# Gated linear attention with interleaved cross-attention: another order of the chains, and repeated gate-logit matmuls in the last two heads

## The reference, cut to what matters

```python
log_a = log_sigmoid(glr @ w_gate2 + b_gate) / 16        # glr: rank 16; this product is the gate logits
b = cumsum(log_a within a chunk of 64); b_ref = b[31]; b_last = b[63]
att = tril((q * exp(b - b_ref)) @ (k * exp(b_ref - b)).T)
o = att @ v + (q * exp(b)) @ state
state = exp(b_last) * state + (k * exp(b_last - b)).T @ v
tok = rms_norm(o) * silu(og)
p = softmax(xq @ k_mem.T / 8); xa = p @ v_mem            # cross-attention
x = x + concat(tok, xa) @ w_out
```

## Time and profile before

| what | value |
|---|---|
| median of 3 runs | 2727.84 us |
| lowest, highest run | 2727.36, 2731.31 us |
| the profiled execution | 2724.89 us, its span 2723.1 us |
| mean granted TensorE clock over the span | 0.977 of full speed |
| TensorE busy | 2603.9 us, 96% of the span |
| VectorE, ScalarE, GpSimd busy | 1317.6, 848.3, 200.5 us |

### The profile page before, as it was taken

The page is one execution under the profiler, slowest core; times in us unless marked ns, Lnnn a source line. Parts: engine busy times, 40 slices in busy tenths (PEclk is TensorE's granted clock), DMA queues, the critical chain, the costliest instruction groups (busy, mean ns, idle before and its releaser), DMA issues. The chain is left out here.

```text
span 2723.1 us, 33041 instructions
## 1 busy us (share of the span) xinstructions
PE 2603.9 (96%) x12444; PEld 2206.9 (81%) x12444; DVE 1317.6 (48%) x2290; ACT 848.3 (31%) x1774; POOL 200.5 (7%) x271
## 2 busy tenths in 40 slices
PE   7998888999999999998999999998899999999999
PEld 7996767878888888887888888787778888888887
DVE  4423453445444544446554562453645544454445
ACT  6434342332222222214425433324333222222221
POOL 1100131000000000001211021111000000000000
PEclk9999978999999999998999999998999999999999
DMA  4221201121111111112102001102421111111111
GB/s 145 87 70 28 87 15 39 39 87 50 51 47 46 51 50 46 46 39 101 47 17 74 32 32 50 59 17 80 154 71 55 47 54 54 46 52 49 46 39 62
DMA packets 165245, 153.88 MB, mean 57 GB/s; under 512 B 32856, under 2 KB 135496, under 8 KB 165128
## 3 DMA queue, kind: packets, MB, share of 16 engines
q1 hardware_dynamic: 160968, 152.31, 17.5%
q10 hardware_dynamic: 4160, 0.02, 0.1%
HBM read 134.69 MB, written 17.61 MB: 56 GB/s over the span
## 5 line engine op out<-in xcount | busy, mean ns | idle before, releaser
L356 PE MATMUL psum<-hT_hi,f_up_hi 128*128 128x512 f32 x1376 | 426.6, 389 | 3.9 <-PEq L562 3.9
L356 PE MATMUL psum<-hT_hi,f_up_lo 128*128 128x512 f32 x1376 | 426.3, 389 | 0.0
L356 PE MATMUL psum<-hT_lo,f_up_hi 128*128 128x512 f32 x1376 | 426.2, 389 | 0.0
L238 DVE TENSOR_TENSOR f_up_lo<-raw,f_up_hi 128x1024 fp32r<-128x1024 f32 x84 | 102.9, 1225 | 489.7 <-ACT f_up_hi L182 489.7
L356 PEld LDWEIGHTS psum<-hT_hi,f_up_hi 128*128 128x128 f32 x1376 | 258.1, 188 | 58.5 <-issue 5.1
L356 PEld LDWEIGHTS psum<-hT_hi,f_up_lo 128*128 128x128 f32 x1376 | 258.3, 188 | 53.7
L356 PEld LDWEIGHTS psum<-hT_lo,f_up_hi 128*128 128x128 f32 x1376 | 258.3, 188 | 53.5
L256 DVE TENSOR_TENSOR XY<-XY,psum 128x512 f32<-128x512 f32 x352 | 234.4, 684 | 113.9 <-PE psum L52 113.7
L182 ACT ACTIVATE f_up_hi<-raw 128x1024 fp32r<-128x1024 f32 x84 | 89.1, 1061 | 613.7 <-PE psum L356 589.0
L50 PE MATMUL psum<-w_hi,hT_hi 128*128 128x512 f32 (+1 forms) x640 | 249.7, 390 | 17.2 <-DVE w_lo L805 10.7
L50 PE MATMUL psum<-f_down_hi,f_act_hi 128*128 128x512 f32 x640 | 249.0, 389 | 0.0
(11 more groups left out here) (289 smaller groups left out, 4055.0 us busy)
## 6 DMA issues: line engine op xcount, KB each, us to landing
raw<-in_ffn_w_up_dram SPq DMA_DIRECT2D x88, 512.0 KB, 3.7
f_down_raw<-in_ffn_w_down_dram SPq DMA_DIRECT2D x22, 1024.0 KB, 4.9
w_raw<-in_b_w_in_dram SPq DMA_DIRECT2D x18, 1024.0 KB, 5.4
w_raw<-in_a_w_in_dram SPq DMA_DIRECT2D x8, 768.0 KB, 5.7
group_out<-stage SPq DMA_DIRECT2D x24, 256.0 KB, 2.1
o_outs<-group_out SPq DMA_DIRECT2D x24, 256.0 KB, 3.7
XY<-in_x_dram SPq DMA_DIRECT2D x8, 512.0 KB, 10.3
w_raw<-in_xa_w_kv_dram SPq DMA_DIRECT2D x8, 512.0 KB, 3.6
```

The costliest lines, as they stand in the source:

```text
L238: nc.vector.tensor_tensor(up_lo[n_slot][:, :, :], up_raw[n_slot], up_hi[n_slot][:, :, :].bitcast(F32), ALU.subtract).then_inc(up_split, 1)
L356: mm = nc.tensor.matmul(psum[:, 2 * j + half, :], w[j][:, d, :], h[:, d, half * HALF:(half + 1) * HALF], start=first, stop=final)
```

## The change

- `CrossUnits`: the output products of a unit go to a bank of the ring in place of bank 3, and each unit (not each two) has its reciprocal and its division. The transposes are in bank 3. The buffers of the probabilities lie in `cross_room`, a piece of SBUF that was the split weights' second buffer, with one still in V.
- `project`: all parts from 2 on use one pair of weight buffers and banks 0 and 1 (before: two pairs, and banks 0, 1 or 2, 3). A part starts after ACT has copied the one before (before: the one two before).
- ACT: `gate` is cut in `gate_in` and `gate_out`, with the copies of the token products between them; a head's odd part is copied and split later, and in head h the cross-attention's exponentials of stage "att" stand behind the copies of the key rows.
- DVE: `cross_pair` and the cross-attention steps of "att" stand ahead of the next head's `sums_of`; `states` and the steps of "state" stand ahead of `product(h + 1, 0)`; the third product stands behind `outputs`.
- TensorE: 4 slices (before 3) of an even part are projected ahead of the gate; the steps of "state" stand ahead of the odd part; cross steps are dealt out 3, 2, 3, 3, 2, 3, 3.
- `fill(n)`: n matmuls of head 0's gate weights with the rank rows into bank 2, which nobody reads: 2, 2, 3 and 3 at four places of head 2 and of head 3, 20 in all.

```diff
-    def pe(self, pe, s):
+    def pe(self, pe, s, ring_wait):
...
-            if i == 0 and t >= 1:
-                pe.wait_ge(self.out_done, t)
+            ring_wait(u)
...
-        CROSS = {(1, "out"): range(0, 3), (2, "att"): range(3, 6), (2, "state"): range(6, 9), (2, "out"): range(9, 12),
-                 (3, "att"): range(12, 14), (3, "state"): range(14, 16), (3, "out"): range(16, CrossUnits.STEPS)}
+        CROSS = {(1, "out"): range(0, 3), (2, "att"): range(3, 5), (2, "state"): range(5, 8), (2, "out"): range(8, 11),
+                 (3, "att"): range(11, 13), (3, "state"): range(13, 16), (3, "out"): range(16, CrossUnits.STEPS)}
...
         @block.vector
...
             product(0, 0)
             product(0, 3)
-            low(3)
             product(0, 1)
             product(0, 2)
             for h in range(GLA_HEADS):
                 more = h + 1 < GLA_HEADS
-                if more:
-                    sums_of(h + 1)
+                fresh = h + 1 < LAST
                 cross_pair(h)
                 cross_steps(cross.dve, dve, h, "att")
                 if more:
+                    sums_of(h + 1)
+                if fresh:
+                    low(2 * h + 3)
+                states(h)
+                cross_steps(cross.dve, dve, h, "state")
+                if more:
                     product(h + 1, 0)
-                states(h)
                 if h + 2 < LAST:
                     low(2 * h + 4)
                 if more:
                     product(h + 1, 1)
-                    product(h + 1, 2)
-                if h + 2 < LAST:
-                    low(2 * h + 5)
-                cross_steps(cross.dve, dve, h, "state")
                 outputs(h)
                 if more:
+                    product(h + 1, 2)
                     product(h + 1, 3)
...
          @block.tensor
...
             def project(s, ds=range(DC)):
-                h, part = divmod(s, 2)
+                w_hi, w_lo = (x[1 if s == 1 else 0] for x in (first_parts.hi, first_parts.lo))
                 if s >= 2:
                     pe.wait_ge(w_split, s - 1)
-                    pe.wait_ge(copied, s - 1)
+                    pe.wait_ge(copied, 1 if s == 2 else s)
...
+            def fill(n):
+
+                for i in range(n):
+                    nc.tensor.matmul(psum[0:DK, 2, :], gate2[:, 0:DK], rank[:, i % 2 * HALF:(i % 2 + 1) * HALF], start=True, stop=True)
+
-            EARLY = 3
+            EARLY = 4
...
             for h in range(GLA_HEADS):
                 if h + 1 < GLA_HEADS:
                     gate(h + 1)
+                if h + 2 > LAST:
+                    fill(2)
                 token_products(h)
                 if h + 1 < LAST:
                     project(2 * h + 2, range(EARLY, DC))
-                cross_steps(cross.pe, pe, h, "att")
+                cross_at(h, "att")
+                if h + 2 > LAST:
+                    fill(2)
                 state_changes(h)
+                cross_at(h, "state")
+                if h + 2 > LAST:
+                    fill(3)
                 if h + 1 < LAST:
                     project(2 * h + 3)
-                cross_steps(cross.pe, pe, h, "state")
                 outputs(h)
...
+                cross_at(h, "out")
                 if h + 2 < LAST:
                     project(2 * h + 4, range(EARLY))
-                cross_steps(cross.pe, pe, h, "out")
+                if h + 2 > LAST:
+                    fill(3)
```

More of the change, by code:

```diff
@@ L1359, in dve @@
         if 0 <= u < self.PAIRS:
+            two = slice(2 * u, 2 * u + 2)
             dve.wait_ge(self.turned, u + 1)
@@ L1478, in source, with enter, enter_cross, part_bank @@
             return (last_rows if h == LAST else qk_rows)[i][0:DK, :, :]
-        first_of, z_of = [], [0]
+        def enter(kind, who, n, h):
+            entry_of[h, kind] = len(ring)
+            ring.extend([(kind, who, h)] * n)
+        def enter_cross(h, stage):
+            for s in CROSS.get((h, stage), ()):
+                u = s - CrossUnits.O_LAG
+                if 0 <= u < CrossUnits.PAIRS:
+                    cross_of[u] = len(ring)
+                    ring.append(("xa", "xa", u))
+        enter("z", "act", 2, 0)
         for h in range(GLA_HEADS):
             if h + 1 < GLA_HEADS:
[L1483 to L1486, removed]
+                enter("z", "act", 2, h + 1)
+            enter("att", "act", 2, h)
+            enter("cross", "dve", 1, h)
+            enter_cross(h, "att")
+            enter("keys", "act", 2, h)
+            enter("delta", "state", 4, h)
+            enter_cross(h, "state")
+            enter("out", "dve", 4, h)
+            enter_cross(h, "out")
+        z_of = [entry_of[h, "z"] for h in range(GLA_HEADS)]
         def freed(i):
-            kind, who = ring[i]
+            kind, who, h = ring[i]
+            if kind == "xa":
+                return cross.out_done, h + 1
             if kind == "delta":
-                h = max(h for h in range(GLA_HEADS) if first_of[h] <= i)
-                return state_ready, (PAIRS - 1) * h + min(2 * (i - first_of[h] - 5) + 2, PAIRS - 1)
-            return (by_act if who == "act" else by_dve), sum(w == who for _, w in ring[:i + 1])
+                return state_ready, (PAIRS - 1) * h + min(2 * (i - entry_of[h, "delta"]) + 2, PAIRS - 1)
+            return (by_act if who == "act" else by_dve), sum(w == who for _, w, _ in ring[:i + 1])
         def bank(i):
             return psum[:, 4 + i % 4, :]
+        def part_bank(s, half):
+            return psum[:, (2 if s == 1 else 0) + half, :]
+        def at(h, kind, i=0):
+            return entry_of[h, kind] + i
         def mixes_before(i):
-            return sum(kind != "z" for kind, _ in ring[:i])
+            return sum(kind not in ("z", "xa") for kind, _, _ in ring[:i])
         block = ctx.enter_context(nc.Block())
@@ L1564, in high @@
             def high(s):
-                h, part = divmod(s, 2)
                 act.wait_ge(w_loaded, 32 * (s - 1))
-                act.wait_ge(projected, s - 1)
-                nc.scalar.activation(parts_hi[part], w_raw, ACT.Copy).then_inc(w_high, 1)
+                act.wait_ge(projected, 1 if s == 2 else s)
+                nc.scalar.activation(first_parts.hi[0], w_raw, ACT.Copy).then_inc(w_high, 1)
             def copy(h, i):
+                first = 2 if h == 0 and i == 1 else 0
                 act.wait_ge(projected, 2 * h + i + 1)
@@ L1626, in _ @@
                     factor(h + 1, 1)
-                    if fresh:
-                        copy(h + 1, 0)
-                if h:
-                    act.wait_ge(squared, PAIRS * h)
-                for i in range(2):
-                    act.wait_ge(mixed, mixes_before(f + 3 + i) + 1)
-                    nc.scalar.activation(k_rows[:, 4 * i:4 * i + 4, :], bank(f + 3 + i)[:, 0:4 * DK].rearrange("p (c k) -> p c k", k=DK),
-                                         ACT.Copy).then_inc(by_act, 1)
+                cross_steps(cross.act, act, h, "state")
+                if more:
+                    factor(h + 1, 2)
+                if fresh:
+                    copy(h + 1, 1)
                 if h + 2 < LAST:
                     high(2 * h + 4)
-                if more:
-                    factor(h + 1, 2)
-                    if fresh:
-                        copy(h + 1, 1)
-                if h + 2 < LAST:
-                    high(2 * h + 5)
-                cross_steps(cross.act, act, h, "state")
                 if h:
```

156 lines of the change are left out of this document (78 added, 78 removed).

## The result

The changed kernel takes **2752.8 us** (median of 4 runs, 2748.9 to 2757.8), the one before 2727.6 (2727.3 to 2731.3) beside it: a ratio of 1.009, 95% interval 1.0077 to 1.0102. It is **25.2 us slower**. The forecast had the sign right but said 10.8, and its range ended at 2744. The profiled execution took 2748.9 us, with a span of 2747.1 against 2723.1.

What follows compares the result with a forecast made beforehand. TensorE, busy nearly all through, was taken to bound the kernel. Heads 0 and 1 gave -5.0 us, the rest -4.8 + 17.2 + 0.7 + 2.7 = +15.8, together +10.8: 2737 us, range 2723 to 2744.

Steps and rivals of the forecast that it cites:

- I take it that the stretches cost what they cost before: Stretches at 1.2 GHz come to as much as before, so 5.5 us possibly gained in heads 2 and 3 is left out.
- warm: Rival: fills count as work and raise the clock in heads 2 and 3; -1.3 to -5.7 us, middle -3.5; chance 0.20.
- The fills' own length: Fills in heads 2 and 3, 0.9 us each at 2.4 GHz, covering no wait: +17.2, and +2.7 for the last three.
- The third product ... up to 1.22 us ... +0.7: Heads 2 and 3: product moved behind `outputs` lengthens the chain the wait of 5.99 hangs on; 0 to 1.22, middle +0.7.
- Heads 0 and 1: Terms up to the start of step 2 sum to -5.0 us (before at 337.96); new waits of 2.9 and twice 1.9.
- -4.7: Heads 0 and 1: clock falls at 257.4 and 308.6 cost 6.4 us and go; 1.7 us given back for new waits.
- if step 2 isn't about 5 us early: Test at the start of step 2: unless about 5 us early, at 333, the whole forecast falls.
- The product ahead of step 2: A product of 1.22 us moves behind `outputs`, into the chain that the wait of 4.98 hangs on: +1.2 us.
- Heads 2 and 3, waits: Waits of 3.60 and 2.04 shorten, the latter to one like 0.81; 1.91 left for the sums: -4.8 us.
- The buffer rival: Rival: one pair of weight buffers makes TensorE wait at parts 3 and 5; +15 us; chance 0.08.
- They fill: Rival: fills stand in waits missed in the reading and cost nothing at fifteen places; -8 us; chance 0.09.
- The next phase's transposes: Sign of being right: the phase after the changed one starts its first transposes at about 444 (before 433.62).

Runs made afterwards that it cites:

- experiment 1: The changed kernel without its 20 fills: 2722.7 us, -4.8 against the kernel before, ratio 0.9981.
- experiment 2: The changed kernel with each fill's operands replaced by ones of 128 rows, same output: 2738.4 us, +10.9 against the kernel before.
- experiment 5: The changed kernel without fills and with GpSimd's splits moved out of head 2: 2711.5 us, -15.6 against the kernel before, ratio 0.994.
- experiment 3: The changed kernel, fills kept, with GpSimd's splits four in head 1 and four in head 3, none in head 2: 2744.8 us, +17.4 against the kernel before.
- experiment 6: The kernel before with only GpSimd's splits moved, as in experiment 3: 2723.3 us, -3.9, ratio 0.9986.
- experiment 4: The changed kernel without the last three fills, behind head 3's last value product: 2750.7 us, +23.2 against the kernel before.
- experiment 8: experiment 5 plus unread 128-row matmuls (twelve, eight, five) in TensorE's three remaining waits: 2715.5 us, -11.6 against the kernel before.
- experiment 9: experiment 5 plus unread 16-row matmuls, places and number as in experiment 8: 2736.1 us, +8.9 against the kernel before.
- experiment 10: experiment 5 plus unread 128-row matmuls in the three waits, only six, four and two: 2710.6 us, -15.6 against the kernel before.
- experiment 11: The changed kernel measured once more, nothing edited: 2754.1 us, +27.8 against the kernel before.
- experiment 12: experiment 5 with VectorE's third and fourth product moved behind the first and second cross step of an out stage: 2709.9 us, -17.7 against the kernel before.
- experiment 7: The changed kernel without fills, third product back ahead of `outputs`, splits unmoved: 2721.5 us, -4.7 against the kernel before.

## Why the prediction was wrong

The forecast was fills +19.9 and order -9.1, together +10.8. Measured: fills +30 to +32.6, order -4.8. It misses by 14.4 us, of which the fills make 10 and the order 4.

**"I take it that the stretches cost what they cost before"** is the step that failed most. The mechanism was seen: flat matmuls don't hold the clock, it falls at the five fills, the token products of head 3 run at 1.2 GHz. All three came true, and the "warm" rival fell with them, at 10.3 and 13.6 us in which TensorE was busy without a gap at half clock. The Trainium skill's "activity releases the throttle" (TensorE: Matmul & The Clock Gate, Part 1: The HAM clock gate) does not fit these two windows either. One sign of "warm" did show: the clock rose at 336.8, just after the gate had begun at 336.50, so the first two fills ran at 2.4 GHz and not at 1.2 as priced. But it fell again at 340.2, with TensorE busy since 333.64. What failed is the price. The term left at zero measures 11 to 14 us by the medians (experiments 1 and 2; 9 by the two profiles of the changed kernel and experiment 1), and the range allowed 6 for it. Twenty flat matmuls make new stretches, and whatever runs in them takes twice as long; priced was only that two fills are slow themselves.

**The fills' own length** was right: 17.2 + 2.7 forecast with the first two at the low clock, 18.6 at 2.4 GHz measured. That they cover nothing was wrong, by a little: the wait for the states, 4.90 without fills, is 2.22 and 1.56 with them, and with the splits moved three waits of 1.00, 1.78 and 1.56 (experiment 5) become one of 0.27 (experiment 3). So the fills and the slower clock behind them cover 1 to 4 us.

**"The third product ... up to 1.22 us ... +0.7"** is the second failed step. The wait went from 5.99 to 9.35, +3.4. With the splits moved it is 3.28 in the old order (experiment 6) and 4.41 in the new one (experiment 3), so the product itself is 1.13 of the 3.4 and the splits are the other 2.2: products now run beside them, where before only the decay copy and the small product behind it did (2.10 and 0.94 us for 0.17 and 0.16). The copy in the trace of before:

```profile
389.76 2.10 DVE L1687 COPY gla_chunk_decay<-gla_q_in 96x16 f32<-96x16 f32 x1
```

I had looked for GpSimd's queue among the things that are moved, but not among those that are met: no group of rows of mine showed its instructions. Experiments 3, 5 and 6 put the collision at 10.8 us in the new order and 3.9 in the old.

**Heads 0 and 1.** Step 2 starts at 333.64 against a forecast of 333, and the waits are 2.93 and twice 1.87 (forecast 2.9 and 1.9). That step 2 came at the forecast time was luck, and as a forecast of the typical run it was wrong. In eleven profiled executions with the same instructions up to there (after, and experiments 1 to 5 and 8 to 12) steps 0 and 1 start between 325.65 and 332.00, on the mean at 329.6, against 331.10 and 331.51 in two executions of the old order. The term of **-4.7** for the clock was drawn from one profile: the old order had 13.6 us at 1.2 GHz in heads 0 and 1, the new one between 3.4 and 17.1. On the mean it is 11.5, worth -1, not -4.7. In the seven of these executions that have the wait of 6.11, step 2 itself starts between 333.64 and 339.99, on the mean at 338.3, where the kernel before had 337.96. By the prediction's own test ("if step 2 isn't about 5 us early") the forecast falls in all but one. The waits that went, of 2.33 and 2.24, and those that came are as forecast.

**The product ahead of step 2**: +1.2 forecast, +1.13 measured (4.98 to 6.11; 4.97 again in experiment 7).

**Heads 2 and 3, waits**: the one before head 2's key rows, 2.04, went to 0.40 where I had 0.8; head 3's was 0.40 before. The wait for the sums stayed at 2.22 and 1.56 in the profile of after; its running sum takes 4.33 us beside the splits, and 2.29 in experiment 5, where the first of the two is 1.78 and the second still 1.56. I had left 1.91 for the second and nothing for the first. The three old waits of 3.60, 2.04 and 1.91 became 2.22, 0.40 and 1.56, which is -3.4 and not -4.8. **The buffer rival** fell: no wait ahead of parts 3 and 5. **"They fill"** fell as a whole: it had fifteen fills for nothing, and they cover the 1 to 4 us above. At the long waits of 6.11 and 9.35 no fill stood.

**The next phase's transposes** were forecast at about 444 and start at 456.8: the sum of the above, 23.2 us behind the old 433.6.

## What to carry to other kernels

Here an unread matmul of 128 rows held the clock and one of 16 rows did not; nothing between was tried. Outside a wait even the tall one cost nearly its length, and the flat one cost its length and let what followed run at half speed. Inside the waits the tall ones gained 1.5 us in the profiled stretch and nothing that the medians separate, since TensorE then reached some of VectorE's results sooner and waited: price the wait together with the clock. It works the other way too: in experiment 12 the waits that went came back as low clock. Before moving a step on VectorE, read what GpSimd runs at its new place; here the place of four splits was worth about as much as the whole reordering (10.8 and 11.8 us).

## What the runs showed of the hardware that I had not expected

- TensorE busy without a gap, with 16-row matmuls, fell from 2.4 to 1.2 GHz after 3.8 us and stayed there for the 13.3 us that they lasted. With 128-row ones of the same output (96x512) it stayed at 2.4 GHz for 10.3 us.
- The same instructions in heads 0 and 1 spent between 3.4 and 17.1 us at 1.2 GHz, from one execution to the next, and step 0 moved by 6.3 us with it. One profile doesn't tell the price of such a stretch. What decides between the patterns wasn't tried.
- VectorE beside GpSimd's splits: a product of two SBUF operands took 3.15 and 3.37 us for 1.22, a running sum 4.33 for 2.29, a copy of 16 elements per partition 1.00 for 0.17, and GpSimd's cast 2.03 for 1.04. Both engines lose.
